# Conformer convolution: the copy through device memory in natural layout, loaded back by one DMA per shift, and the convolutions one projection unit later

## The reference, cut to what matters

```
def conformer_conv(h, w_pw1, b_pw1, w_dw, b_dw, ln_g, ln_b, w_pw2, b_pw2):
    a, gate = jnp.split(h @ w_pw1 + b_pw1, 2, axis=-1)
    u = a * jax.nn.sigmoid(gate)
    dw = lax.conv_general_dilated(
        u, w_dw[:, None, :], window_strides=(1,), padding=((CONV_WIDTH - 1, 0),),
        dimension_numbers=('NWC', 'WIO', 'NWC'), feature_group_count=D_MODEL) + b_dw
    ... (a layer norm over the 1024 channels, silu) ...
    return z @ w_pw2 + b_pw2
```

## Time and profile before

| | us |
|---|---|
| median of 3 executions | 1229.38 |
| profiled execution, its own time | 1229.8 |
| its span, first to last instruction | 1227.9 |
| TensorE matmuls busy | 1145.9 (93%) |
| VectorE busy | 844.3 (69%) |
| ScalarE busy | 611.5 (50%) |
| mean granted TensorE clock | 0.965 of full |

### The profile page before, as it was taken

How to read it: one execution, slowest core, us unless ns; L and a number is a source line. 1 busy time by engine, 2 the same in 40 slices (tenths; PEclk the granted TensorE clock), 3 DMA queues, 4 the chain that set the end, 5 groups by cost and what they waited for, 6 DMA issues and landing times.

```text
span 1227.9 us, 18649 instructions
## 1 busy us (share of the span) xinstructions
PE 1145.9 (93%) x7262; PEld 1002.0 (82%) x7262; DVE 844.3 (69%) x1319; ACT 611.5 (50%) x953; POOL 31.4 (3%) x52
## 2 busy tenths in 40 slices
PE   8999999999566369999999999999999989999998
PEld 8998888888354149888889999888888758888887
DVE  6868877765543037877765886777766788877753
ACT  6536565644321036565644345565544566656541
POOL 0120000000000000000000000000000210000000
PEclk9999999999887669999999999999999999999999
DMA  7533555554444414455555354555554403555452
GB/s 287 207 138 137 178 200 176 207 192 161 115 104 108 107 31 160 172 196 181 206 179 199 139 206 172 178 200 178 202 200 176 171 35 104 187 191 201 177 206 69
DMA packets 31143, 203.57 MB, mean 166 GB/s; under 512 B 3536, under 2 KB 5840, under 8 KB 7632
## 3 DMA queue, kind: packets, MB, share of 16 engines
q1 hardware_dynamic: 30768, 202.24, 47.7%
q10 hardware_dynamic: 288, 0.14, 0.1%
HBM read 200.14 MB, written 2.23 MB: 165 GB/s over the span
## 4 chain that ended last, share of the span: by engine, by line
PE 85%; DMA 5%; DVE 4%; issue 3%; ACT 1%; POOL 0%; SPq 0%; DVEq 0%; ACTq 0%
PE banks L381 39%; PE banks L387 20%; PE banks L359 5%; PE banks L362 5%; PE banks L365 5%; PE banks L420 5%; DMA shifts<-scr 3%; DVE lo_t L290 1%; DMA raw_t<-w 1%; PE banks L403 1%; PE banks L409 1%; PE banks L406 1%; DMA scr<-shifts 1%; ACT hi_t L284 0%; PE banks L1444 0%
## 5 line engine op out<-in xcount | busy, mean ns | idle before, releaser
L290 DVE TENSOR_TENSOR lo_t<-raw_t,hi_t 128x1024 fp32r<-128x1024 f32 x368 | 444.9, 1220 | 9.1 <-ACT hi_t L284 7.6
L284 ACT ACTIVATE hi_t<-raw_t 128x1024 fp32r<-128x1024 f32 x368 | 381.0, 1049 | 67.2 <-PE banks L387 24.7
L381 PE MATMUL banks<-x,hi_t 128*128 128x512 f32 x1536 | 389.3, 393 | 0.5 <-DVE x L315 0.5
L381 PEld LDWEIGHTS banks<-x,hi_t 128*128 128x128 f32 x1536 | 275.3, 189 | 50.2 <-ACT x L311 0.9
L387 PEld LDWEIGHTS banks<-x,lo_t 128*128 128x128 f32 x1536 | 211.7, 190 | 16.5
L387 PE MATMUL banks<-x,lo_t 128*128 128x256 f32 x1536 | 216.6, 282 | 0.0
L381 PE MATMUL banks<-f,hi_t 128*128 128x512 f32 x704 | 181.3, 393 | 0.9 <-DVE f L505 0.9
L381 PEld LDWEIGHTS banks<-f,hi_t 128*128 128x128 f32 x704 | 124.8, 189 | 22.9 <-issue 2.6
L420 PE MATMUL banks<-scr 128*32 128x256 f32 (+5 forms) x656 | 70.2, 482 | 62.6 <-DMA scr<-shifts 31.9
L509 DVE TENSOR_TENSOR scr<-banks,scr 128x512 f32<-128x512 f32 x88 | 60.8, 691 | 84.3 <-ACT scr L561 83.5
L420 PEld LDWEIGHTS banks<-scr 128*32 128x32 f32 (+3 forms) x656 | 38.5, 152 | 89.4 <-issue 80.0
(11 more groups left out here) (181 smaller groups left out, 1115.5 us busy)
## 6 DMA issues: line engine op xcount, KB each, us to landing
raw_t<-w SPq DMA_DIRECT2D x183, 1024.0 KB, 4.9
scr<-shifts SPq DMA_DIRECT2D x8, 574.5 KB
shifts<-scr SPq DMA_DIRECT2D x8, 144.0 KB
raw_t<-w SPq DMA_DIRECT2D x2, 512.0 KB, 7.6
out<-h SPq DMA_DIRECT2D x8, 128.0 KB, 3.8
cst<-consts SPq DMA_DIRECT2D x1, 816.0 KB, 11.7
h<-xT SPq DMA_DIRECT2D x1, 768.0 KB, 7.9
h<-xT SPq DMA_DIRECT2D x1, 256.0 KB, 4.6
```

The costliest lines, as they stand in the source:

```text
L284: e.activation(hi_t[:, p % RING, :], raw_of(p), ACT.Copy).then_inc(s_hi, 1)
L290: e.tensor_tensor(lo_t[:, p % RING, :], raw_of(p), hi_t[:, p % RING, :].bitcast(F32), ALU.subtract).then_inc(s_lo, 1)
L381: e.matmul(halves(banks[:, to[j], :]), hi_t[:, slot, r * P:(r + 1) * P], parts[:, ks[j], :, :], start=ks[j] == 0, stop=False, skip_group_c ...
```

## The change

Seven edits, all in the Conformer stage:

- SP: `load_stack(u)` now stands ahead of chunk 52 + u instead of behind it.
- The tensor in device memory is 8 x 128 x 288, written by rows of the natural order: one DMA with the pattern [128, 288] on both sides.
- The read is four DMAs, one per shift j, each to 32 partitions: source pattern [32, 4, 284], in runs of 1136 bytes. The semaphore is waited for at 64 instead of 16 per use.
- The stack buffers are 4 x 284 wide instead of 4 x 288.
- TensorE: convolutions 0 and 1 stand behind unit 4, the shift and convolutions 2 and 3 behind unit 6.
- ScalarE: the squares of tiles 0 to 3 move from unit 5 to unit 6.
- VectorE: the takes and the shift move with them; the diagonals of units 3 to 6 are built behind the take that stands two before them, those of 7 where they were.

```
             for c in range(RAW, w.shape[0]):
-                load_chunk(e, c)
                 if 0 <= c - G_PW1 // 16 - 5 < KD:
                     load_stack(e, c - G_PW1 // 16 - 5)
+                load_chunk(e, c)
...
-        US_C, NU = 288, 3
+        US_C, SW, NU = 288, 284, 3
...
-        stack = [scratch(C3 + n * 4 * US_C, 4 * US_C) for n in range(NS)]
-        C4 = C3 + NS * 4 * US_C
+        stack = [scratch(C3 + n * 4 * SW, 4 * SW).rearrange("p (a b) -> p a b", a=4) for n in range(NS)]
+        C4 = C3 + NS * 4 * SW
...
             e.wait_ge(s_cu, u + 1)
-            by_row = bass.AP(shifts, u * 32 * 4 * US_C, [[US_C, 4], [4 * US_C, 32], [1, US_C]])
-            e.dma_start(by_row, u_r[u % NU]).then_inc(s_kept, 16)
+            e.dma_start(shifts[u], u_r[u % NU]).then_inc(s_kept, 16)
             if u >= NS:
                 e.wait_ge(s_conv, u - NS + 1)
             e.wait_ge(s_kept, 16 * (u + 1))
-            again = bass.AP(shifts, u * 32 * 4 * US_C, [[1, 4], [4 * US_C, 32], [1, 4 * US_C - 3]])
-            e.dma_start(stack[u % NS][:, 0:4 * US_C - 3], again).then_inc(s_stack[u % NS], 16)
+            for j in range(4):
+                again = bass.AP(shifts, u * P * US_C + j, [[US_C, 32], [32 * US_C, 4], [1, SW]])
+                e.dma_start(stack[u % NS][32 * j:32 * j + 32, :, :], again).then_inc(s_stack[u % NS], 16)
...
-                if u == 3:
+                if u == 4:
                     pe_conv(e, 0)
                     pe_conv(e, 1)
-                if u == 5:
+                if u == 6:
                     e.wait_ge(s_dw, 2)
...
-            e.wait_ge(s_stack[u % NS], 16 * (u // NS + 1))
+            e.wait_ge(s_stack[u % NS], 64 * (u // NS + 1))
...
-                    last = plain(e, out_g, diags[u % NS][:, g, m, :], stack[u % NS][:, g * US_C + 4 * m:g * US_C + 4 * m + T], m == 0, m == 7)
+                    last = plain(e, out_g, diags[u % NS][:, g, m, :], stack[u % NS][:, g, 4 * m:4 * m + T], m == 0, m == 7)
... (ScalarE)
-                if u == 5:
+                if u == 6:
                     hi_to(e, c + 11)
                     squares(0, 2)
... (VectorE)
-                if u not in (5, 7):
+                if u < 3:
                     diagonals(u)
-                if u == 3:
+                if u == 4:
                     take(0)
+                    diagonals(3)
                     take(1)
-                if u == 5:
+                    diagonals(4)
+                if u == 6:
                     e.wait_ge(s_cpart, 1)
...
                     take(2)
                     diagonals(5)
                     take(3)
+                    diagonals(6)
...
-    shifts = nc.dram_tensor("shifts", (8, 32, 4, 288), _mybir.dt.float32, kind="Internal")
+    shifts = nc.dram_tensor("shifts", (8, 128, 288), _mybir.dt.float32, kind="Internal")
```

## The result

The changed kernel takes 1169.86 us (median of 4 executions, 1168.07 to 1175.06), the kernel before 1229.24 us: ratio 0.9523, 95% interval 0.9489 to 0.9557. 1171 was predicted, with 1158 to 1192 as the range. Run again beside the experiments it took 1173.2 us against 1228.3, ratio 0.9549 (0.9536 to 0.9562). The profiled execution took 1171.39 us, span 1169.5.

What follows compares the result with a forecast made beforehand. SP's loop of stack writes and reads, 16.1 us per unit on four of sixteen DMA engines, was taken to bound the stage. At 9.0 us the first output matmul moves from 452.26 to 393.9: 1229.8 less 58.4, 1171 us, range 1158 to 1192.

Steps and rivals of the forecast that it cites:

- π: New time per unit of SP's loop in the Conformer stage: 9.0 us (7.9 to 10.1), against 16.1 before.
- W: Time from a stack write's issue on SP to its landing, a chunk just ahead: 6.0 us (4.9 to 7.1).
- The reads: Four stack reads per unit on SP: all landed 3.8 us after the first issue, against 9.9 for one before.
- The sum's steps: Conformer stage: chunk 56, shift, convolution 3, unit 7, convolutions 4 to 7, first output matmul at 393.9, 58.4 us sooner.
- The bounds 388.4 and 399.4: First output matmul's time with W at 4.9 (kernel 1166 us) and at 7.1 (1177 us).
- the other chain: SP's write 7, its landing, reads, cold convolution, output: ends last above π = 10, at 330.5 + 7π.
- Convolutions one unit later: TensorE: unit 4 fills the 9.5 us stand before convolution 0; worth nothing by itself while SP paces.
- Four fixed costs in a row: Rival: each stack read takes its own 1.9 us, π 14.1, kernel 1210 us; chance 0.07, in-between outcomes included.
- All engines but slower: Rival: stack transfers use all engines at a lower rate, 215 GB/s, π 12, kernel 1192 us; chance 0.24.
- TensorE as the bound: Rival: nothing stands in TensorE's way from 317.7, first output matmul at 378.0, kernel 1155 us; chance 0.05.
- Slower than before: Rival: slow stack reads push π past 17.4, 1241 us at 50 GB/s; chance 0.04, shared with unchanged.
- Four engines after all: Rival: new stack patterns still run on four engines, loop near 16 us, 1225 to 1240; chance 0.04, shared with slower.

Runs made afterwards that it cites:

- the best of the experiments: Changed kernel with one read of 128 partitions (32 outermost, 4596-byte runs) and VectorE's shift behind unit 5's product, against the kernel before: 1158.48 us, ratio 0.9431.

## Why the prediction was right

*The mechanism* was right and is shown: the read on four of sixteen engines, because of an outermost 4. The kernel with nothing but that dimension moved (ratio 0.9549), the one with everything but the transfers changed (1.0018) and the one with the transfers alone (0.9549) leave no part of the gain to the order of the work. The Trainium skill's rule on the outermost dimension ("DMA: Bandwidth & Descriptors", "Rules for kernel authors") is borne out by 3.6 us against 9.9 for the same bytes and runs. On the write the prediction was incomplete: it treated the two patterns as one cause, and the read's alone gives the whole of this change's gain.

*The loop.* π was put at 9.0 and measured 8.95 in the profiled execution (9.2 in the second). That it fits so well is luck: two errors cancel. W was 6.0 and measured 6.1, 8.1, 5.5, 6.7, 6.2 and 7.7, mean 6.7, two of the six above the bound of 7.1. The issues were 3.0, four times the spacing of one read of before and a chunk, and 0.46 for the chunk; measured from 320.49 to 322.75, 2.3. An issue of the new pattern takes 0.44, not 0.63.

*The reads* were to land 3.8 us after the first issue, paced by the issues. Each took 2.9 us to land, not 1.9, at 242 GB/s with nearly all engines busy, so that the four were there some 4.3 us after the first issue (an estimate: the last issue comes 1.3 us behind the first, and the landing takes 3.0). That was mis-sized, and it cost nothing visible, but narrowly: stack 7 landed at about 380.8 by the same estimate and convolution 7 began at 381.5. Four reads against a single large one was the objection that the prediction raised against the change, and it holds: one read landed in 3.8 us, needed three issues fewer, and the kernel was 10 us faster.

*The sum's steps*, predicted and measured: chunk 56 landed 356.9, 356.4; convolution 3 began 359.6, 358.8, cold as said (6.45); unit 7 ended 371.5, 371.0; convolutions 4 to 7 without a stand; output 393.9, 392.7. Within this, chunk 52 was to be issued at 315.3 and to land 5.6 us later, a term for which the prediction names no row; it was issued at 313.98 and split at 320.09, 6.1 later against 320.9 predicted, again two errors that cancel. The bounds 388.4 and 399.4 don't follow from the formulas. With W at 4.9 the sum gives 389.5 (1167 us); with 7.1, π is 10.1, where by the prediction's own words the other chain ends last, and 330.5 + 7π gives 401.1 (1179 us). And the stand before convolution 3 was to be 9 us and was 11.1 and 13.1. None of these moves the forecast itself. ScalarE's list waited for chunks as predicted:

```profile
320.09 1.06 ACT L284 ACTIVATE hi_t<-raw_t 128x1024 fp32r<-128x1024 f32 x1 [7.66 <-DMA raw_t<-w]
...
356.41 1.06 ACT L284 ACTIVATE hi_t<-raw_t 128x1024 fp32r<-128x1024 f32 x1 [5.53 <-DMA raw_t<-w]
```

*Convolutions one unit later* were put at nothing by themselves: measured about 1 us. I said that chunk 56 would then hold the shift, which it did. What I did not see is that this stand costs nothing as long as SP's loop is 9 us (0.9555 without most of it), and perhaps 4 us when it is 7.3.

*The rivals.* Four fixed costs in a row: excluded, four reads are issued in 1.75 us and overlap. All engines but slower: the reads were slower than I said, the loop wasn't. TensorE as the bound (1155): not in this kernel, with 11 us of stand left; the best of the experiments, at 1158.48, comes near it. Slower than before: only without the new transfers, and by 2 us. Four engines after all: excluded by the share of 0.98.

## What to carry to other kernels

Where a DMA is on a waiting path, read its share of the engines while it is alone: 0.25 of sixteen is four, and a swap of two dimensions in the pattern may be most of the remedy. Do it for every transfer on the path: here the read gave some 55 us, and the write on sixteen engines seems to be worth 10 more once the read is one DMA. Then look for the second chain before removing a stand: a stand of 10 us taken away gained nothing while the loop beside it took 9 us. When an edit changes several things, run each alone; here the edits to the transfers carried everything, a smaller one gained as much, and a single read in place of the four gained 10 us more.

## What the runs showed beyond that

- A DMA confined to four engines also holds back what is spread over all: in the kernel before, the chunk behind each such read landed 13.2 to 14.5 us after its issue, where the median chunk takes 4.9.
- A 144 KB write to device memory lands in 1.8 us alone and in 5.5 to 8.1 behind four reads and a 1 MB load. From GpSimd's queue, with the loads on SP's, the wait behind the issue was 5.3 to 7.0 in the five cases with a load under way, and 2.9 and 3.2 behind reads alone.
- 581 KB in four DMAs of 1136-byte runs to 32 partitions each went at 242 GB/s in a microsecond with nearly all engines busy (share 0.98), one DMA of 4596-byte runs to 128 partitions, with a chunk behind it, at 271 and 376. Whether the length of the runs or the 32 partitions does it was not separated.
